# Memory norm, keys and values of two attention layers moved ahead of the first feed-forward

## The chip, the cores and the metric

One core of a Trainium2 chip runs the whole kernel. Its engines work side by side, each through its own queue of instructions in order: TensorE (matmuls), VectorE, ScalarE, GpSimd and SyncE (SP, which only issues DMAs). They wait for each other and for transfers by semaphores. The metric is the time of one execution on the device in microseconds; lower is better.

## The reference

The input is 512 tokens of width 1024. A first block adds a mixer of four branches and a feed-forward of width 4096, both behind norms with shift and scale from a conditioning vector. A second block of two layers follows. Each of its layers reads, beside the tokens, a fixed memory of 256 tokens:

```python
for layer in range(DEPTH_2):
    xn = rmsnorm(h, norm_mix[layer])
    mn = rmsnorm(mem, norm_mem[layer])
    ...                     # q, k, v, qm from xn; mix = attention of 12 heads
    mem_out = memory_attention(split_heads(qm, N_MEM_HEADS), mn, w_mem_kv[layer])
    heads = jnp.concatenate([mix, mem_out], axis=1)
    h = h + merge_heads(heads) @ w_out[layer]
    h = h + conv_ffn(rmsnorm(h, norm_ffn[layer]), w_up[layer], conv_w[layer],
                     conv_b[layer], w_down[layer])

def memory_attention(qm, mem_n, w_mem_kv):
    km, vm = jnp.split(mem_n @ w_mem_kv, 2, axis=-1)
    ...                     # softmax(qm km / sqrt(64)) vm, 4 heads of 64
```

`mem` does not depend on `x`. Layer 0 uses attention with forget gates, layer 1 a dilated attention with rotated queries and keys.

## The kernel before

Activations lie transposed: channels on the 128 partitions, tokens along the row, in 8 blocks (`KT`). Weights come as a stream of 334 pieces of 128x1024, one per output tile of 128 channels. Each matmul operand is split in a high and a low part, so a product of one block is three matmuls (high with high, high with low, low with high) and a tile is 24 matmuls of 512 columns. For the memory the columns are 256.

**Weights.** GpSimd loads them into four slots. `load_high(q)` waits until an older piece has been used (`w_used`) and issues a 512 KB DMA. `load_low(q)` waits for that to land, writes its negative into `w_lo`, and issues a second 512 KB DMA that adds the full weights to it. In the queue, `load_high(q + 2)` stands between `load_low(q)` and `load_low(q + 1)`. TensorE's `open_piece` waits for the low part. The order of pieces is fixed by `layout`.

**TensorE's order** is written out by hand: `project(tiles, owner, ...)` makes tiles one after the other in four PSUM banks in turn; `owner` names the semaphore that says when a bank has been read. `modulation(g)` is eight one-column matmuls that sum a weight column over partitions. `total_squares` is one matmul with ones, which sums squares for a norm.

**Between mixer and feed-forward.** VectorE's `mixer_update(k)` adds output tile k to x and then calls `modulate`, which scales two pieces of the modulation weights (`in_ada`, 512 KB each, 16 of them here, brought by SP into four slots, each when the piece four before it has been used). When all are through, TensorE makes `modulation(4)` and the sum of squares, ScalarE the root (`rms_x`), VectorE the reciprocal (`norm_start`) and the eight blocks of the norm, which ScalarE (high part) and VectorE (low part) finish, and the first feed-forward tile follows.

**The memory.** SP loads it (1 MB, `memT`) once before the attention of layer 0 and again after it, into the room of the softmax rows. In the last group of the first feed-forward, and in the last group of layer 0's, ScalarE squares it, VectorE adds the squares, and one `total_squares` sums them. In the head of each attention layer VectorE makes the norm (`memory_norm`: three operations per block, 24 in all), and TensorE makes two key tiles and two value tiles (`HEAD_PIECES`: memq0, memq1, q0, k0, v0, memk0, memk1, memv0, memv1). Values must have tokens on the partitions, so `turn` transposes each value tile with TensorE into bank 7 from a copy by ScalarE (`value_copy`), and VectorE takes it (`value_taken`). In layer 0 VectorE then turns the forget logits into running sums (`forget_parts`). Only when the last memory value has been taken does `attention` begin: 32 units (8 of the memory heads first), each with scores, row maximum, exponent, division, transpose and output, with the remaining 15 projections fed in between. Units of 12 heads read the forget rows that SP copies to `g_lo`.

## Time and profile before

| | |
|---|---|
| time, median of 3 runs | 2319.56 us (2309.91 to 2321.72) |
| span of the profiled execution | 2315.7 us |
| TensorE busy | 2147.8 us, 93% |
| VectorE, ScalarE, GpSimd busy | 56%, 20%, 37% |
| mean granted TensorE clock | 0.957 of full |
| DMA | 393.60 MB, mean 170 GB/s |

The profile has several views. The page gives the busy time of each engine and the chain of work that ended last. The chain of waits goes back from the last instruction to what released each. The timeline lists instructions with the idle time before each and what ended it. The windows give busy times, the granted clock and DMA traffic of a stretch. Times are microseconds from the start of the span.

### The profile page before, as it was taken

The numbers are of one execution on the slowest core, as the hardware profiler recorded it, in microseconds if no ns is written. First come the engines' busy times: TensorE is split into PE (matmuls) and PEld (weight loads), VectorE is DVE, ScalarE is ACT, GpSimd is POOL, SyncE is SP. The second block draws the span as 40 slices with busy tenths as digits, with TensorE's granted clock in tenths as the row PEclk, the third lists the DMA queues.
The fourth block names the chain that finished last, engine by engine and source line by source line (L and its number), as shares of the span: only waits on it lengthen the run. The fifth ranks groups of instructions, "written<-read, shape, count | busy, mean of one in ns | idle before, by whom it ended". The sixth has DMA issues, their size and how long they took to land.

```text
span 2315.7 us, 27377 instructions
## 1 busy us (share of the span) xinstructions
PE 2147.8 (93%) x10790; PEld 1703.9 (74%) x10790; DVE 1296.3 (56%) x1824; ACT 456.1 (20%) x839; POOL 846.9 (37%) x1009
## 2 busy tenths in 40 slices
PE   6889798998799999989989999999899989999996
PEld 5668586676588888866767878787766668878784
DVE  6775655436763243674444745637636747727274
ACT  2112301210100000313342211113133432102011
POOL 1323233232244444432214444444432224444442
PEclk7999899997799999999999999999999989999998
DMA  8867577576799999985528989898965449899885
GB/s 280 221 141 167 114 151 145 121 181 161 229 236 196 196 192 193 192 174 115 108 57 194 194 184 195 179 200 187 197 136 101 92 102 186 178 198 191 184 193 141
DMA packets 121783, 393.60 MB, mean 170 GB/s; under 512 B 25220, under 2 KB 27396, under 8 KB 121272
## 3 DMA queue, kind: packets, MB, share of 16 engines
q0 software_dynamic: 96624, 350.46, 71.3%
q1 hardware_dynamic: 25032, 41.39, 5.6%
q8 instruction: 86, 1.41, 0.3%
q14 instruction: 41, 0.34, 0.1%
HBM read 387.92 MB, written 3.92 MB: 169 GB/s over the span
## 4 chain that ended last, share of the span: by engine, by line
PE 74%; DVE 14%; DMA 7%; issue 2%; ACT 1%; POOL 1%; SPq 0%; DVEq 0%; ACTq 0%; POOLq 0%
PE ps L1582 62%; DMA w_lo<-in_w 4%; PE ps L1710 2%; DMA arena<-in_ada 2%; PE ps L1611 2%; PE ps L1739 2%; PE ps L1725 1%; DVE work L668 1%; PE ps L1896 1%; DVE g_lo L462 1%; POOL w_lo L429 1%; DVE arena L556 1%; DVE arena L669 1%; DMA w_hi<-in_w 1%; DVE small L855 1%
## 5 line engine op out<-in xcount | busy, mean ns | idle before, releaser
L1582 PE MATMUL ps<-h_hi,w_hi 128*128 128x512 f32 x1760 | 711.1, 404 | 27.1 <-DVE h_lo L512 13.3
L1582 PE MATMUL ps<-h_hi,w_lo 128*128 128x512 f32 x1760 | 690.1, 392 | 0.0
L1582 PE MATMUL ps<-h_lo,w_hi 128*128 128x512 f32 x1760 | 690.0, 392 | 0.0
L424 POOL DMA_DIRECT2D w_hi<-in_w x334 | 187.4, 561 | 1289.9 <-PE ps L1582 1203.3
L1582 PEld LDWEIGHTS ps<-h_hi,w_hi 128*128 128x128 f32 x1760 | 332.6, 189 | 126.2 <-issue 29.9
L1582 PEld LDWEIGHTS ps<-h_hi,w_lo 128*128 128x128 f32 x1760 | 332.8, 189 | 71.3
L1582 PEld LDWEIGHTS ps<-h_lo,w_hi 128*128 128x128 f32 x1760 | 333.4, 189 | 64.8 <-issue 2.2
L429 POOL TENSOR_SCALAR w_lo<-w_hi 128x1024 fp32r<-128x1024 f32 x334 | 359.5, 1076 | 45.3 <-DMA w_hi<-in_w 39.8
L1582 PE MATMUL ps<-g_hi,w_hi 128*128 128x512 f32 (+1 forms) x792 | 313.8, 396 | 28.6 <-DMA w_lo<-in_w 19.5
L432 POOL DMA_DIRECT2D w_lo<-in_w x334 | 301.0, 901 | 106.0 <-POOL w_lo L429 106.0
L1582 PE MATMUL ps<-g_lo,w_hi 128*128 128x512 f32 (+1 forms) x792 | 307.1, 388 | 0.0
L1582 PE MATMUL ps<-g_hi,w_lo 128*128 128x512 f32 (+1 forms) x792 | 306.8, 387 | 0.0
L1582 PEld LDWEIGHTS ps<-g_hi,w_hi 128*128 128x128 f32 x792 | 153.0, 193 | 66.8 <-DMA w_lo<-in_w 24.9
L1582 PEld LDWEIGHTS ps<-g_hi,w_lo 128*128 128x128 f32 x792 | 153.1, 193 | 29.8
L1582 PEld LDWEIGHTS ps<-g_lo,w_hi 128*128 128x128 f32 x792 | 153.3, 194 | 28.2 <-issue 0.5
L1540 ACT ACTIVATE arena<-arena,vec 128x512 f32<-128x512 f32 x88 | 71.8, 816 | 404.6 <-DVE arena L901 401.4
L915 DVE TENSOR_TENSOR x<-ps,x 128x512 f32<-128x512 f32 x48 | 33.2, 692 | 170.2 <-PE ps L1582 159.1
L906 DVE SCALAR_TENSOR_TENSOR arena<-arena,vec 128x511 f32<-128x511 f32 x88 | 115.4, 1311 | 3.3 <-ACT arena L1540 0.3
L901 DVE TENSOR_TENSOR arena<-ps,work 128x512 f32<-128x512 f32 x88 | 60.9, 692 | 89.9 <-PE ps L1582 88.5
L1170 DVE TENSOR_TENSOR arena<-arena 128x512 f32<-128x512 f32 x32 | 51.4, 1606 | 72.2 <-ACT arena L1461 72.2
L1178 DVE SCALAR_TENSOR_TENSOR x<-ps,mod,x 128x512 f32<-128x512 f32 x32 | 24.0, 751 | 102.2 <-PE ps L1582 102.1
L461 DVE CAST g_hi<-arena 128x512 fp32r<-128x512 f32 (+1 forms) x100 | 76.3, 763 | 3.4
(373 smaller groups left out, 2080.1 us busy)
## 6 DMA issues: line engine op xcount, KB each, us to landing
w_hi<-in_w POOLq DMA_DIRECT2D x334, 512.0 KB, 4.0
w_lo<-in_w POOLq DMA_DIRECT2D x334, 512.0 KB, 5.8
arena<-in_ada SPq DMA_DIRECT2D x40, 512.0 KB, 9.4
x<-in_ada SPq DMA_DIRECT2D x8, 512.0 KB, 7.9
x<-in_xT SPq DMA_DIRECT2D x1, 2048.0 KB, 10.0
x<-in_xT SPq DMA_DIRECT2D x4, 512.0 KB, 4.4
arena<-in_memT SPq DMA_DIRECT2D x2, 1024.0 KB, 7.1
out_y<-arena SPq DMA_DIRECT2D x4, 512.0 KB, 2.6
```

Of the source, the lines that this page charges most:

```text
L424: pool.dma_start(w_hi[:, q % SLOTS, :], A["w"][q]).then_inc(S(f"high_in{q % SLOTS}"), 16)
L429: pool.tensor_scalar(w_lo[:, q % SLOTS, :], w_hi[:, q % SLOTS, :].bitcast(F32), -1.0, 0.0, ALU.mult, ALU.add).then_inc(S("negated"), 1)
L432: pool.dma_start(w_lo[:, q % SLOTS, :], A["w"][q], accum_op=ALU.add).then_inc(S(f"low_in{q % SLOTS}"), 16)
L461: do(dve.tensor_copy(hi, src))
L901: do(dve.tensor_tensor(cv_m["z"][:, side, :], tile()[:], rstd, ALU.mult), "conv_scaled")
L906: do(dve.scalar_tensor_tensor(dst[:, 1:], z[:, :T - 1], w(1), dst[:, 1:], ALU.mult, ALU.add))
L1170: do(dve.tensor_tensor(s, r, r, ALU.mult), "relu_used")
L1540: do(act.activation(c[:, j % 2, :], cv_m["z"][:, side, :], ACT.Identity, scale=V("cw2", at), bias=V("cb2", 44 * layer + 22 * side + j0 + j ...
L1582: mm = pe.matmul(bank, w[:, slot, cols], a(k), start=(k == 0 and i == 0), stop=(k == blocks - 1 and i == 2))
L1611: mm = pe.matmul(banks[i], w[:, slots[i], cols], a(k), start=(k == 0 and j == 0), stop=(k == blocks - 1 and j == 2))
L1710: mm = pe.matmul(ps[2 + g][:, 0:width], at_m["q"][half(g), pair, P * qb:P * qb + P], keys, start=True, stop=not fox)
L1739: mm = pe.matmul(ps[6][64 * g:64 * g + 64, P * qb:P * qb + P], values, at_m["pt"][:, u % 2, g, P * b:P * b + P], start=(b == 0), stop=(b = ...
```

## The change

The memory norm, keys and values of both layers are made once, between the output projection of the mixer and the first feed-forward. Their eight weight pieces move to that place in the stream; the number of pieces stays 334.

- SP loads the memory once, behind four modulation pieces and before x is loaded again.
- ScalarE makes eight squares (128x256), TensorE adds them up by eight matmuls with ones, before the output projection. ScalarE then writes 16 high parts (memory times gain), VectorE 16 low parts, three per `mixer_update`. The norm's root is not applied to them: keys are multiplied by it on VectorE, in the first feed-forward group; for values it is brought from a row to a column (`diag`, `mem_row`) and given as the scale of ScalarE's copy.
- Values are made with the memory as the stationary operand and the weights as the moving one (`memory_values`), so they come out with tokens on the partitions, and are not transposed.
- The heads of the attention lose the memory norm and four tiles. The transpose of v0 moves into the first unit.

```diff
-HEAD_PIECES = ["memq0", "memq1", "q0", "k0", "v0", "memk0", "memk1", "memv0", "memv1"]
+HEAD_PIECES = ["memq0", "memq1", "q0", "k0", "v0"]
...
             for q in range(24, 24 + ADA):
                 ada_piece(q, ada_m["ada"])
+            sp.dma_start(mem_in, A["memT"]).then_inc(S("mem_in"), 16)
...
-            sp.wait_ge(S("ada_used"), 48 - ADA_PE)
-            sp.dma_start(mem_in, A["memT"]).then_inc(S("mem_in"), 16)
             sp.wait_ge(S("forget_parts"), 1)
-            sp.wait_ge(S("taken"), TURNED[0].index("memv1") + 1)
+            sp.wait_ge(S("x_done"), 8 + 8 * FF_GROUPS)
...
             sp.wait_ge(S("heads"), NP + NMP)
-            sp.dma_start(mem_in, A["memT"]).then_inc(S("mem_in"), 16)
             sp.dma_start(masks, A["mask_dil"]).then_inc(S("mask_in"), 16)
... VectorE
             def memory_root():
+
                 need("rms_ready")
                 do(dve.reciprocal(mem_rstd, mem_rstd))
+                for i in range(2):
+                    do(dve.tensor_tensor(mem_m["diag"], mem_rstd[:, P * i:P * i + P], K("ident"), ALU.mult))
+                    do(dve.tensor_reduce(mem_row[:, i:i + 1], mem_m["diag"], AX.X, ALU.add), "mem_row")
+
+            def memory_low(i):
+
+                layer, k = i // KT, i % KT
+                need("mem_high")
+                do(dve.scalar_tensor_tensor(mn(g_lo, layer, k), mem_in[:, k, :], V("g_mem2", 8 * layer + k), mn(g_hi, layer, k).bitcast(F32),
+                                            ALU.mult, ALU.subtract), "mem_ready")
...
-                for k in range(KT):
-                    memory_norm(k)
...
-                value_scaled("v0")
-                for i in range(NMP):
-                    do(dve.tensor_copy(km[:, i, :], tile()[:, 0:MT]), "dve_freed")
-                    if i == 0:
-                        value_taken("v0")
...
-                skip(2)
-                for i in range(NMP):
-                    value_taken(f"memv{i}")
+                value_scaled("v0")
...
             def mixer_update(k):
                 do(dve.scalar_tensor_tensor(x[:, k, :], tile()[:], mod[:, 16 + k:17 + k], x[:, k, :], ALU.mult, ALU.add), "x_done")
+                for i in range(3 * k, min(3 * k + 3, 2 * KT)):
+                    memory_low(i)
+                if k == 2:
+                    memory_root()
                 modulate(3 + k // 4, 2 * (k % 4), 2 * (k % 4) + 2)
...
-                    if last:
-                        add_square(j, mem_sq, mem_total)
+                    if first and j < 2 * NMP:
+                        keys = mem_keys[j // NMP][:, j % NMP, :]
+                        dve.wait_ge(S("mem_copied"), 2 * N_KV)
+                        do(dve.tensor_tensor(keys, keys, mem_rstd, ALU.mult), "mem_scaled")
... ScalarE
+            act.wait_ge(S("mem_in"), 16)
+            for k in range(KT):
+                if k >= MEM_SQ:
+                    act.wait_ge(S("mem_square_used"), k - MEM_SQ + 1)
+                do(act.activation(mem_sq(k), mem_in[:, k, :], ACT.Square), "mem_square")
+            act.wait_ge(S("tile"), n.value["tile"])
+            for layer in range(2):
+                for k in range(KT):
+                    do(act.activation(mn(g_hi, layer, k), mem_in[:, k, :], ACT.Identity, scale=V("g_mem2", 8 * layer + k)), "mem_high")
+            act.wait_ge(S("mem_square_used"), KT)
+            do(act.activation(mem_rstd, PB[:, 0:MT], ACT.Sqrt, bias=small[:, 38, 0:1], scale=1.0 / D), "rms_ready")
             skip(8)
             rms_x(0)
-            high_shifted(lambda k: mod[:, 24 + k:25 + k])
+            for i in range(NMP):
+                keys_copy(0, i)
+            values_copy(0)
...
+            for k in range(KT):
+                high2(k)
+                if k in (1, 3):
+                    keys_copy(1, k // 2)
+            values_copy(1)
... TensorE
+            for k in range(KT):
+                pe.wait_ge(S("mem_square"), k + 1)
+                pe.matmul(PB[:, 0:MT], K("ones"), mem_sq(k), start=(k == 0), stop=(k == KT - 1)).then_inc(S("mem_square_used"), 1)
             project(7, "x_done", ready=lambda k: need("merged"))
             modulation(3)
             project(1, "x_done")
+            pe.wait_ge(S("mem_ready"), 2 * KT)
+            project(1, "mem_copied", operand=memory[0], width=MT)
             modulation(4)
+            total_squares(work[:, 2, :])
+            project(NMP - 1, "mem_copied", operand=memory[0], width=MT)
+            memory_values(0)
+            project(NMP, "mem_copied", operand=memory[1], width=MT)
+            memory_values(1)
...
-            total_squares(work[:, 2, :])
...
-                project(1, "dve_freed", operand=mem, width=MT, ready=lambda k: need("mem_ready"))
-                turn("v0", layer)
-                project(NMP - 1, "dve_freed", operand=mem, width=MT)
-                for i in range(NMP):
-                    project(1, "v_copied", operand=mem, width=MT)
-                    if i:
-                        turn(f"memv{i - 1}", layer)
-                turn(f"memv{NMP - 1}", layer)
-                attention(layer)
+                attention(layer, ready)
```

In three places the order of instructions shows what moves. The first is TensorE at the end of the output projection, before (L1647 is the modulation sum, L1663 the sum of squares, the rows behind them the first feed-forward tile):

```order
L1582 MATMUL ps<-h_lo,w_hi 128x512
L1582 MATMUL ps<-h_hi,w_lo 128x512
L1647 MATMUL ps<-con,arena 128x1 x8
L1663 MATMUL ps<-work,con 128x512
L1582 MATMUL ps<-h_hi,w_hi 128x512
```

The same place now. The rows from the first piece are the end of memk0 of layer 0, in the second the first values of the memory (L1681) follow memk1:

```order
L1585 MATMUL ps<-g_lo,w_hi 128x256
L1585 MATMUL ps<-g_hi,w_lo 128x256
L1650 MATMUL ps<-con,arena 128x1 x8
L1666 MATMUL ps<-work,con 128x512
L1585 MATMUL ps<-g_hi,w_hi 128x256
```

```order
L1585 MATMUL ps<-g_hi,w_hi 128x256
L1585 MATMUL ps<-g_lo,w_hi 128x256
L1585 MATMUL ps<-g_hi,w_lo 128x256
L1681 MATMUL ps<-w_hi,g_hi 128x256
L1681 MATMUL ps<-w_lo,g_hi 128x256
L1681 MATMUL ps<-w_hi,g_lo 128x256
```

One memory tile stands before the modulation, seven behind it and before the feed-forward tile. The second place is VectorE in the same stretch, before (L1153 adds a tile to x, L556 scales modulation weights):

```order
L1153 SCALAR_TENSOR_TENSOR x<-ps,mod,x 128x512
L556 SCALAR_TENSOR_TENSOR arena<-arena,small 128x1024 x2
L469 TENSOR_TENSOR work<-work 128x512
L1153 SCALAR_TENSOR_TENSOR x<-ps,mod,x 128x512
L556 SCALAR_TENSOR_TENSOR arena<-arena,small 128x1024 x2
```

and now, at the third tile (L506 is `memory_low`, L497 to L500 `memory_root`, L566 scales modulation weights):

```order
L1137 SCALAR_TENSOR_TENSOR x<-ps,mod,x 128x512
L506 SCALAR_TENSOR_TENSOR g_lo<-arena,vec,g_hi 128x256 x3
L497 RECIPROCAL arena<-arena 128x256
L499 TENSOR_TENSOR arena<-arena,con 128x128
L500 TENSOR_REDUCE small<-arena 128x1
L499 TENSOR_TENSOR arena<-arena,con 128x128
L500 TENSOR_REDUCE small<-arena 128x1
L566 SCALAR_TENSOR_TENSOR arena<-arena,small 128x1024 x2
```

The memory's low parts stand between the update of x and the modulation weights. The third place is TensorE in the head of layer 0. Before, the end of memv1 and its transposes (L1676) stand ahead of the first scores (L1710):

```order
L1582 MATMUL ps<-g_lo,w_hi 128x256
L1582 MATMUL ps<-g_hi,w_lo 128x256
L1676 MATMUL ps<-con,arena 128x128 x4
L1710 MATMUL ps<-arena 128x256 x4
L1582 MATMUL ps<-h_hi,w_hi 128x512
```

Now the end of v0 stands there, and the transposes of v0 (L1701) come in the first unit:

```order
L1585 MATMUL ps<-h_lo,w_hi 128x512
L1585 MATMUL ps<-h_hi,w_lo 128x512
L1737 MATMUL ps<-arena 128x256 x4
L1585 MATMUL ps<-h_hi,w_hi 128x512
...
L1701 MATMUL ps<-con,arena 128x128 x4
L1752 MATMUL ps<-con,arena 128x128 x4
```

The scores follow v0 directly.

## Rows read from the trace of the kernel before

**Rows 1.** The page, parts 1 and 4: engines, and the chain that ended last.

```profile
PE 2147.8 (93%) x10790; PEld 1703.9 (74%) x10790; DVE 1296.3 (56%) x1824; ACT 456.1 (20%) x839; POOL 846.9 (37%) x1009
...
PE 74%; DVE 14%; DMA 7%; issue 2%; ACT 1%; POOL 1%; SPq 0%; DVEq 0%; ACTq 0%; POOLq 0%
```

**Rows 2.** Chain of waits, mixer to feed-forward: start, duration, what released the next.

```profile
598.78 10.76 DMA arena<-in_ada
...
609.63 1.28 DVE arena L556
...
611.11 3.57 PE ps L1647 x16
614.68 1.93 PE ps L1663 x2
...
617.48 3.37 DVE work L505
...
627.53 57.14 PE ps L1582 x234
```

**Rows 3.** Windows: busy time of each engine (instructions), clock, DMA share, GB/s.

```profile
610.00:615.00 5.00, 3.89 (x17) 3.89 (x18) 2.54 (x6) 0.00 (x0) 0.00 (x0) 0.50 1.01 339
...
1035.00:1040.00 5.00, 2.85 (x23) 2.40 (x21) 4.17 (x7) 0.38 (x1) 2.33 (x3) 1.00 1.01 214
1040.00:1045.00 5.00, 1.30 (x6) 0.61 (x6) 0.89 (x3) 2.41 (x5) 0.00 (x0) 0.51 0.66 113
...
1620.00:1625.00 5.00, 4.52 (x21) 3.41 (x20) 3.69 (x5) 2.24 (x4) 2.95 (x4) 1.00 0.90 208
```

**Rows 4.** Timeline of layer 0's head: start, duration, engine, line, [idle before].

```profile
1008.26 1.42 DVE L761 SCALAR_TENSOR_TENSOR arena<-ps,work 128x512 f32<-128x512 f32 x2
...
1017.44 0.39 PE L1582 MATMUL ps<-h_hi,w_lo 128*128 128x512 f32 x1
...
1031.03 1.77 DVE L823 TENSOR_SCALAR work<-work 12x512 f32<-12x512 f32 x1
...
1037.94 0.68 DVE L832 TENSOR_TENSOR work<-work 12x512 fp32r<-12x512 f32 x1
...
1041.64 0.69 DVE L855 TENSOR_REDUCE small<-ps 128x2 f32<-128x512 f32 x1 [1.48 <-PE ps L1710]
```

**Rows 5.** Timeline of layer 1's head: rotation of k0, first row maximum.

```profile
1668.17 1.02 PE L1673 MATMUL ps<-arena,con 128*128 128x512 f32 x2
...
1691.48 0.69 DVE L855 TENSOR_REDUCE small<-ps 128x2 f32<-128x512 f32 x1 [1.19 <-PE ps L1710]
```

**Rows 6.** Chain of waits at the mixer's end: low weights land, three tiles.

```profile
496.61 8.95 DMA w_lo<-in_w
...
505.59 16.62 PE ps L1582 x72
```

**Rows 7.** Chain of waits, both heads: transposes of v0, memory tiles.

```profile
1024.61 1.11 PE ps L1676 x4
...
1676.91 0.23 PE ps L1582
...
1685.32 3.13 PE ps L1582 x24
```

**Rows 8.** Timeline: the column sum of the memory's squares.

```profile
1607.07 0.59 PE L1663 MATMUL ps<-arena,con 128*128 128x256 f32 x2
```

**Rows 9.** Timeline: ScalarE's first square of x, VectorE's first memory operation.

```profile
566.54 0.63 ACT L1231 ACTIVATE work<-x 128x512 f32<-128x512 f32 x1 [42.12 <-issue]
...
1009.71 0.48 DVE L801 SCALAR_TENSOR_TENSOR arena<-arena,vec 128x256 f32<-128x256 f32 x1
```

**Rows 10.** Timeline of GpSimd: loads of high weights, first and last of five.

```profile
1619.85 0.55 POOL L424 DMA_DIRECT2D w_hi<-in_w  x1 [1.09 <-PE ps L1582]
...
1639.87 0.56 POOL L424 DMA_DIRECT2D w_hi<-in_w  x1 [1.84 <-PE ps L1582]
```

**Rows 11.** Windows: beside the four modulation pieces at the mixer's end.

```profile
495.00:498.00 3.00, 3.00 (x15) 2.49 (x14) 2.93 (x3) 0.00 (x0) 1.90 (x2) 1.00 0.97 354
```

More of the change, by code:

```diff
@@ L136, in turned_pieces @@
 def turned_pieces(layer):
-    return [name for name in HEAD_PIECES + BESIDE_PIECES if name[0] == "v" or name[:4] == "memv" or (layer and name[0] in "qk")]
+    return [name for name in HEAD_PIECES + BESIDE_PIECES if name[0] == "v" or (layer and name[0] in "qk")]
 TURNED = [turned_pieces(layer) for layer in range(2)]
@@ L169, in bank_of @@
         return tile % BANKS
-    pieces = n_block1 + sum(n + N_KV + 8 + 2 * FF2 + 8 * len(FF2_GROUPS) for n in (N_FOX, N_DIL))
+    pieces = n_block1 + sum(n + 8 + 2 * FF2 + 8 * len(FF2_GROUPS) for n in (N_FOX, N_DIL))
     with ExitStack() as ctx:
@@ L1663, in total_squares, with memory_values @@
                 pe.matmul(bank[:, 0:width], K("ones"), acc, start=True, stop=True).then_inc(S("squares_total"), 1)
+            def memory_values(layer):
+                at = [bank_of(t[0] + i) for i in range(2)]
+                for b in at:
+                    pe.wait_ge(S(freed[b][0]), freed[b][1])
+                for k in range(KT):
+                    if k % 4 == 0:
+                        slot = open_piece()
+                    hi, lo = mn(g_hi, layer, k), mn(g_lo, layer, k)
+                    cols = slice(MT * (k % 4), MT * (k % 4) + MT)
+                    for i in range(2):
+                        tokens = slice(P * i, P * i + P)
+                        for j, (a, w) in enumerate(((hi, w_hi), (hi, w_lo), (lo, w_hi))):
+                            mm = pe.matmul(ps[at[i]][:, 0:NMP * P], a[:, tokens], w[:, slot, cols], start=(k == 0 and j == 0),
+                                           stop=(k == KT - 1 and j == 2))
+                            if k % 4 == 0 and i == 0 and j == 0:
+                                mm.then_inc(S("w_used"), 1)
+                        if k == KT - 1:
+                            mm.then_inc(S("tile"), 1)
+                            freed[at[i]] = ("mem_copied", n.next("mem_copied"))
+                t[0] += 2
             def turn(name, layer):
                 i, base = TURNED[layer].index(name), TURNED_BASE[layer]
[L1668 removed]
+                kind = lambda other: "rope_copied" if other[0] in "qk" else "v_scaled"
                 pe.wait_ge(S(kind(name)), sum(kind(other) == kind(name) for other in sum(TURNED[:layer], []) + TURNED[layer][:i + 1]))
@@ L1708, in scores @@
                     for g in range(2):
-                        keys = at_m["k"][half(g), pair, 0:width] if pair < NP else at_m["km"][half(g), pair - NP, :]
+                        keys = at_m["k"][half(g), pair, 0:width] if pair < NP else mem_keys[layer][half(g), pair - NP, :]
                         mm = pe.matmul(ps[2 + g][:, 0:width], at_m["q"][half(g), pair, P * qb:P * qb + P], keys,
@@ L2029, in _ @@
                     two_products(pairs, *g, "x_done", hidden)
-                    if layer == 0 and group == len(FF2_GROUPS) - 1:
-                        total_squares(mem_total, MT)
                     project(6, "x_done", operand=g, blocks=pairs)
@@ L2104, in layout @@
     stream.append(pieces_of(first["w_o"]))
+    for layer in range(2):
+        kv = i["w_mem_kv_2"][layer]
+        stream += [pieces_of(kv[:, :NMP * P]), kv[:, NMP * P:].reshape(2, 4, P, NMP * P).transpose(0, 2, 1, 3).reshape(2, P, D)]
     for g in range(FF_GROUPS):
```

111 lines of the change are left out of this document (45 added, 66 removed).

## The prediction

> **What bounds the kernel now.** I read the page first: TensorE is busy 93% of the span, and one matmul line is most of the chain that ended last [rows 1]. So only what opens or closes an idle stretch of TensorE moves the end. The chain of waits and the timeline show three such stretches that the change touches. The first lies between the mixer's output projection and the feed-forward. The last modulation weight is used up at 609.63 + 1.28 = 610.9 us, sixteen small matmuls and the sum of squares follow until 616.6, then a square root and a reciprocal, and the first feed-forward tile is fed block by block until the unbroken run that starts at 627.53 [rows 2]. The clock falls to its lower level there, 0.50 in the windows [rows 3]. The other two are the heads of the attention layers. VectorE makes the memory norm there, and TensorE has 256-column products and transposes between the last value projection and the first scores: 1017.8 to 1041.6 in layer 0 [rows 4], 1669.2 to 1691.5 in layer 1 [rows 5]. The change takes the memory work out of the second and third and puts it in the first.
>
> **Gain 1, the head of layer 0.** The first row maximum of the scores starts at 1041.64 [rows 4]. Afterwards v0 still ends about 1017.8, its last matmul going out at 1017.44, and the first scores can follow it. VectorE then decides. The memory queries are scaled at 1009.7 and q0 right behind them. k0's tile ends one tile pitch, 16.62 / 3 = 5.54 us [rows 6], before v0, so it is scaled at about 1013. Behind it the forget chain stands unchanged, from 1031.03 to 1037.94 + 0.68, so 7.6 us [rows 4], and then v0's scaling, 0.7. That is 1013.0 + 7.6 + 0.7 = 1021.3: the forget chain takes the memory norm's place. Gain 1041.6 − 1021.3 = **20.3 us**. Bounds 18 (k0 half a tile later) and 21.5 (the chain's first step took 1.77 us, its neighbours under 0.7 for the same shape).
>
> **Gain 2, the head of layer 1.** The first row maximum starts at 1691.48. The rotation of k0 on TensorE ends at 1668.17 + 1.02 = 1669.2 [rows 5]. VectorE then has its three operations and v0's scaling, four of 0.7 us, so 1672.1. Gain **19.4 us**, bounds 18 and 20.
>
> **What the attention gets in return.** The transpose of v0 now stands in the first unit. Four such transposes took 1.11 us at the lower clock [rows 7], about half at the higher. TensorE is packed in the later units, so I charge 0.6 per layer, **1.2 us**. The value transposes of the memory are inside the gains. Of the column sums of the memory's squares two go, shown at 0.59 us each [rows 8]: **−1.0 us** in all. Eight of that width come in before the output projection, at most 4.7 us. I take them as free: TensorE is fed block by block by VectorE there, and ScalarE is idle for 42.12 us before its first square [rows 9], which holds 8 squares and 16 scaled copies of some 0.5 us each, 12 us. Were that cover gone, they would cost the 4.7.
>
> **Cost 1, VectorE during the output projection.** It gets 16 operations of 128x256 at 0.48 us [rows 9], a reciprocal of half the width of one that took 3.37 us [rows 2], and four short ones: some 11 us. Part of that falls in waits for modulation weights. But each of their transfers starts only when a slot has been used, and lands 10.76 us later [rows 2], so a late use is a late landing. Walking the sixteen pieces through with that latency, the modulation ends 4.5 us later, at about 615.5. Bounds 2 and 7.
>
> **Cost 2, eight more tiles in the first stretch.** Before, the 234 matmuls end at 627.53 + 57.14 = 684.7 [rows 2]. Nine whole tiles at 5.5 back from there, the first feed-forward tile ends at 635.2. Afterwards TensorE has one keys tile in the idle time, a wait to 615.5, then modulation and squares, 3.57 + 1.93 at the lower clock [rows 2] and half of it at the higher, so about 620. Then come seven memory pieces and the feed-forward tile. 24 matmuls of 256 columns take 3.13 us [rows 7], so the matmuls alone would be through by 642, the feed-forward tile by 647. What decides is the weights, since a memory piece brings as many bytes as any other and has half the matmul time. In layer 1's head a load is released at 1676.91, when the piece two ahead starts, and its own matmuls start at 1685.32 [rows 7]: 8.4 us for two pieces, 4.2 each. In the tail of the last feed-forward group, where many loads follow each other, five loads of high weights are issued between 1619.85 and 1639.87 [rows 10], 5.0 us apart, with the DMA engines 90% busy [rows 3]. I take 4.6 per piece, the middle, since the first of the seven are half loaded and the later ones queue. The feed-forward tile then starts at 620 + 7 x 4.6 = 652, less about 1.5 for the pieces already there, and ends at 656. Cost 656 − 635 = **21 us**, cost 1 within it. Bounds: 12 (matmul time alone, 647) and 26 (5.0 per piece, VectorE at its worst bound). ScalarE puts its copies of keys and values among the norm's high parts. Behind the second keys copy it has four of these to make, some 7 us with VectorE's steps between them, and TensorE has two value pieces for as long, so the norm stays covered.
>
> **Cost 3, the memory load beside the mixer's end.** The 1 MB transfer now queues on SP behind four modulation pieces. Low weights took 8.95 us to land there and TensorE waited for them [rows 6], at 354 GB/s [rows 11]. At that rate 1 MB is 3.0 us. The stretch behind it has some slack, so **1.5 us**, bounds 0 and 3.5. The second memory load, at the end of layer 0, goes. TensorE hardly waits for weights there: 0.3 us gained.
>
> **The sum.** 20.3 + 19.4 + 1.0 + 0.3 − 1.2 − 21 − 1.5 = 17.3 us gained. Against the profiled span of 2315.7 that gives 2298.4. The median of the timed runs lies 3.9 us above that span: 2319.6 − 17.3 = **2302.3 us**.
>
> **Rivals.**
> (a) The supply is no limit: pieces come 4.0 us apart or less and the clock is back at once. The first stretch costs 14, the gain is 24, the time 2295 us. For it: the 8.4 us for two pieces. Against it: only four memory pieces stood in a row there.
> (b) The stretch is dearer: 5.0 or more per piece, VectorE 7 us late, and the memory load costs 3.5. Then 26 + 3.5 leave a gain of 10, 2309 us. For it: modulation pieces of the last group load beside the weights until about 620.
> (c) Bursts at the lower clock. TensorE works 3.1 of 4.6 us while it waits for weights. If the clock stayed at its lower level, a piece would take 5.2 us, which hides the supply, and the stretch would cost 0.5 x 7, some 3 us more: 2306. Against it: the clock was 1.00 in a window with 2.85 of 5 us busy and fell only in the next, with 1.30 [rows 3].
> The Trainium skill, "TensorE: Matmul & The Clock Gate", section "HAM oscillation — how this bites in real kernels", has a kernel whose bursts behind DMA waits each start at the lower clock. [...]
> (d) Slower. The four weight slots work as one: in GpSimd's queue the low part of a piece waits behind the high load of the next, which waits for a piece to start, so every piece pays the whole 8.4 us of the layer 1 row. The tile then starts at 620 + 7 x 8.4 = 679 and ends at 684, a cost of 49, 2330 us. It decides from 6.9 us per piece, where the stretch costs the 38 us that are gained elsewhere. Against it: in the row itself two pieces were under way, and the tail shows 5.0.
> (e) The attention doesn't start earlier, held by a bank, by q0 or by the forget rows. The memory units use no forget rows, and banks 2 and 3 are free when q0 and k0 are scaled, by 1013. Ten us later in both layers than I say, and 2322 is the time.
>
> **How the numbers follow.** The forecast, a gain of 13 to 21 us: 0.53. (a) 0.15, (b) 0.16, (c) 0.07, (d) 0.04, (e) 0.05. A measurement of this kernel can tell about 0.5%, 11.6 us, from no change. Faster by more: the forecast, (a), (c) and a little of (b), 0.77. Within it: most of (b) and (e), 0.18. Slower: the worst of (d) and (e), 0.05. The range from 2293 to 2311 takes in the forecast, (c), nearly all of (a) and most of (b). Its ends are the bounds of the supply and of the memory load.
>
> **What would show it.** Right: the first feed-forward tile ends near 656; memory pieces start 4.2 to 5.0 us apart, waiting for low weights; the modulation ends near 615; the first row maxima come some 20 us earlier, counted from the last v0 matmul. Wrong: an unbroken run from 642 (a), pieces over 7 us apart (d), ScalarE's high parts ending last before the feed-forward, or scores that wait for something other than VectorE's scaling of v0.

## The result: 0.5% faster, near what was forecast

The changed kernel takes 2302.67 us (median of 7 runs, 2298.59 to 2311.46), beside 2318.42 us for the kernel before (7 runs, 2309.91 to 2321.72). The ratio is 0.9945, with a 95% interval of 0.993 to 0.996. The forecast was 2302.3 us. A second measurement of the same kernel gave 0.9947 (0.9928 to 0.9967). Taken as a ratio, the gain is 12.8 us (9 to 16), less than the 17.3 us of the sum.

In the profiled executions the spans are 2300.9 us after and 2315.7 us before. The page's parts 1 and 4, the rows that answer [rows 1]:

```profile
PE 2139.9 (93%) x10794; PEld 1703.4 (74%) x10794; DVE 1272.2 (55%) x1775; ACT 462.3 (20%) x850; POOL 850.3 (37%) x1009
...
PE 77%; DVE 12%; DMA 7%; issue 1%; ACT 1%; POOL 1%; SPq 0%; DVEq 0%; ACTq 0%; POOLq 0%
```

TensorE is busy for 7.9 us less and the span is 14.8 us shorter, so about half of the gain is idle time that went. VectorE's share of the chain fell from 14% to 12%.

**The heads gave what they were to give.** Timeline of VectorE and TensorE in layer 0's head, of the changed kernel (start, duration, engine, line, operation, [idle before]). These rows answer [rows 4]:

```profile
1037.59 0.39 PE L1585 MATMUL ps<-h_hi,w_lo 128*128 128x512 f32 x1
...
1033.37 1.81 DVE L813 TENSOR_SCALAR work<-work 12x512 f32<-12x512 f32 x1
...
1039.43 0.68 DVE L822 TENSOR_TENSOR work<-work 12x512 fp32r<-12x512 f32 x1
1040.14 0.69 DVE L788 TENSOR_TENSOR arena<-ps,work 128x512 f32<-128x512 f32 x1
1040.87 0.69 DVE L843 TENSOR_REDUCE small<-ps 128x2 f32<-128x512 f32 x1
```

The first row maximum (L843) starts 1040.87 − 1037.98 = 2.9 us behind the end of v0's last matmul. Before it was 1041.64 − 1017.83 = 23.8. That is 20.9 us gained. In all eleven profiles of the changed kernel and its variants this distance is 2.7 to 2.9 us. As forecast, the forget chain (L813 to L822) and v0's scaling (L788) now decide. In layer 1, the rows that answer [rows 5]:

```profile
1671.51 1.02 PE L1698 MATMUL ps<-arena,con 128*128 128x512 f32 x2
...
1674.84 0.69 DVE L788 TENSOR_TENSOR arena<-ps,work 128x512 f32<-128x512 f32 x1
1675.57 0.69 DVE L843 TENSOR_REDUCE small<-ps 128x2 f32<-128x512 f32 x1
```

From the end of k0's rotation to the row maximum it is 3.0 us (in all eleven profiles), where it was 22.3: 19.3 us gained.

**The first stretch took over half of it.** Chain of waits of the changed kernel from the modulation to the first feed-forward tile (start, duration, what released the next), which answers [rows 2]:

```profile
599.62 12.11 DMA arena<-in_ada
...
611.83 1.28 DVE arena L566
...
613.30 1.95 PE ps L1650 x16
615.25 1.33 PE ps L1666 x2
...
619.04 6.66 DMA w_lo<-in_w
...
626.46 5.89 DMA w_hi<-in_w
...
633.94 7.38 DMA w_lo<-in_w
...
644.68 5.34 DMA w_lo<-in_w
650.02 0.04 issue
650.06 10.04 PE ps L1585 x43
```

Before, this chain ran through the norm on VectorE. Now it is mostly a chain of weight loads. TensorE's timeline shows the same from its side. Seven tiles follow the first piece behind the modulation: six of the memory and the first of the feed-forward. Five of them start with a wait for low weights.

```profile
625.74 0.42 PE L1681 MATMUL ps<-w_hi,g_hi 128*128 128x256 f32 x1 [2.24 <-DMA w_lo<-in_w]
635.67 0.39 PE L1585 MATMUL ps<-g_hi,w_hi 128*128 128x256 f32 x1 [2.35 <-DMA w_lo<-in_w]
641.46 0.36 PE L1681 MATMUL ps<-w_hi,g_hi 128*128 128x256 f32 x1 [1.16 <-DMA w_lo<-in_w]
645.05 0.38 PE L1681 MATMUL ps<-w_hi,g_hi 128*128 128x256 f32 x1 [0.48 <-DMA w_lo<-in_w]
650.06 0.50 PE L1585 MATMUL ps<-h_hi,w_hi 128*128 128x512 f32 x1 [1.89 <-DMA w_lo<-in_w]
```

The seven memory pieces behind the modulation start at 615.65, and the feed-forward tile at 650.06: (650.06 − 615.65) / 7 = 4.9 us for each. Windows of the same stretch (busy time of each engine, granted clock, DMA share, GB/s):

```profile
620.00:630.00 10.00, 7.76 (x53) 7.55 (x52) 2.32 (x3) 0.38 (x1) 4.98 (x6) 0.83 0.97 224
630.00:640.00 10.00, 7.65 (x51) 7.43 (x50) 7.33 (x8) 4.23 (x7) 5.21 (x6) 0.83 0.95 230
640.00:650.00 10.00, 6.54 (x51) 5.95 (x49) 6.18 (x7) 4.22 (x7) 5.34 (x6) 1.00 0.91 189
```

The DMA engines are over nine tenths busy and TensorE is not. From the last matmul of the output projection to the first feed-forward tile's start it is 650.06 − 606.10 = 44.0 us. Before it was 635.2 − 5.5 − 607.06 = 22.6, with the tile's end as the prediction worked it out: 21.4 us dearer.

**The books of the two traces.** In the profiled execution of the changed kernel the recurrence in front ended 4.1 us earlier (−4.1), though no edit touches what runs before it. Then: the mixer's end +3.1, the first stretch +21.4, layer 0's head −20.9, layer 0 from the first scores to layer 1's rotation +4.1, layer 1's head −19.3, the rest +1.1. That makes −14.6; the spans differ by 14.8. The −4.1 and the +4.1 are taken up below, at the changed kernel's second measurement.

### The profile page after: what moved, and what is told of

Read it like the earlier page. It is cut to its first block, busy times and chain, and to the rows that moved or that the text cites. A ratio compares the mean times of both kernels' runs of the same rounds, so it can differ in the third digit from the quotient of the medians.

```text
span 2300.9 us, 27327 instructions
## 1 busy us (share of the span) xinstructions
PE 2139.9 (93%) x10794; PEld 1703.4 (74%) x10794; DVE 1272.2 (55%) x1775; ACT 462.3 (20%) x850; POOL 850.3 (37%) x1009
## 3 DMA queue, kind: packets, MB, share of 16 engines
q0 software_dynamic: 96624, 350.46, 70.6%
## 4 chain that ended last, share of the span: by engine, by line
PE 77%; DVE 12%; DMA 7%; issue 1%; ACT 1%; POOL 1%; SPq 0%; DVEq 0%; ACTq 0%; POOLq 0%
PE ps L1585 64%; DMA w_lo<-in_w 4%; PE ps L1737 2%; PE ps L1614 2%; PE ps L1766 2%; PE ps L1752 1%; DMA arena<-in_ada 1%; DVE work L678 1%; PE ps L1924 1%; DMA w_hi<-in_w 1%; POOL w_lo L428 1%; DVE arena L566 1%; DMA x<-in_xT 1%; DVE arena L679 1%; DVE work L468 1%
## 5 line engine op out<-in xcount | busy, mean ns | idle before, releaser
L1585 PE MATMUL ps<-g_hi,w_hi 128*128 128x512 f32 (+1 forms) x760 | 305.8, 402 | 27.8 <-DMA w_lo<-in_w 20.7
L1585 PE MATMUL ps<-g_lo,w_hi 128*128 128x512 f32 (+1 forms) x760 | 299.5, 394 | 0.0
L1585 PE MATMUL ps<-g_hi,w_lo 128*128 128x512 f32 (+1 forms) x760 | 299.2, 394 | 0.0
L1585 PEld LDWEIGHTS ps<-g_hi,w_hi 128*128 128x128 f32 x760 | 147.6, 194 | 64.9 <-DMA w_lo<-in_w 24.9
L1585 PEld LDWEIGHTS ps<-g_hi,w_lo 128*128 128x128 f32 x760 | 147.5, 194 | 30.4
L1585 PEld LDWEIGHTS ps<-g_lo,w_hi 128*128 128x128 f32 x760 | 148.1, 195 | 29.1 <-issue 0.8
L1476 ACT ACTIVATE arena<-ps 128x512 f32<-128x512 f32 x32 | 19.2, 600 | 289.6 <-PE ps L1585 289.6
```

Source lines behind the costliest of these rows:

```text
L1585: mm = pe.matmul(bank, w[:, slot, cols], a(k), start=(k == 0 and i == 0), stop=(k == blocks - 1 and i == 2))
```

## Experiments

All ratios are to the kernel before, run beside it on the same chip, with 95% intervals. The gain against the changed kernel is (0.9946 − ratio) x 2316 us, 0.9946 being the mean of its two measurements.

| kernel | median us | ratio | less than changed kernel, us |
|---|---|---|---|
| changed kernel, again | 2301.61 | 0.9947 (0.9928 to 0.9967) | 0 |
| no_pieces | 2283.02 | 0.9869 (0.985 to 0.9888) | 17.8 |
| no_loads | 2292.66 | 0.9908 (0.9887 to 0.9929) | 8.8 |
| few_matmuls | 2303.78 | 0.9955 (0.9942 to 0.9969) | −2.1 |
| half_low | 2297.38 | 0.9918 (0.9893 to 0.9943) | 6.5 |
| mem_late | 2298.72 | 0.9929 (0.9912 to 0.9946) | 3.9 |
| keys_first | 2295.46 | 0.9916 (0.9902 to 0.9931) | 6.9 |
| lows_early | 2302.73 | 0.9945 (0.9927 to 0.9963) | 0.2 |
| two_edits | 2295.55 | 0.9904 (0.988 to 0.9929) | 9.7 |
| all_three | 2296.75 | 0.992 (0.9905 to 0.9935) | 6.0 |

### Loads or matmuls? no_pieces, no_loads, few_matmuls

The theory (W): the weight supply sets the pace of the stretch. The rivals: TensorE's matmuls, some at the lower clock, set it (M), or the norm on VectorE and ScalarE does (N). no_loads takes the eight memory pieces' weights out of the stream and runs all matmuls on weights that lie in a slot already (the part for the values is shown):

```diff
-                    if k % 4 == 0:
-                        slot = open_piece()
+                    slot = (piece[0] - 1) % SLOTS
```

few_matmuls keeps all loads and runs one of eight blocks of 128 rows of each keys piece, and two of the eight of each pair of values pieces:

```diff
-                for k in range(KT):
+                for k in (0, 4):
```

no_pieces does both.

> The changed kernel without the eight memory pieces of the weight stream, and with 3 or 6 matmuls per memory tile instead of 24; everything else (squares, high and low parts, copies, banks) stays. It leaves out the memory's keys and values, so its time shows what the pieces cost and nothing of the result. Theory W (the stretch is paced by weights): the first feed-forward tile is then held by the norm alone, whose last block follows the modulation (613.3) by some 24 us, so the tile ends near 640 instead of 655.5, and the time falls by 13 to 18 us against the changed kernel, to 2285 to 2290. Rival N (ScalarE's copies among the high parts hold the norm, which was complete only at 647.9): the tile ends at 650 or later, and the time falls by less than 6 us.

> The changed kernel with all memory matmuls, which read the slot of the last output projection piece instead of weights of their own; eight pieces fewer are loaded. Its keys and values are wrong, the work on TensorE is the same. Theory W: memory tiles follow each other every 3.1 us from 615.7 (lower clock at the start apart), are done by 640, and the feed-forward tile ends at 645 to 648: 8 to 11 us less than the changed kernel, 2292 to 2295. Rival M (matmul time and the lower clock are the cost, weights are not): within 3 us of the changed kernel, 2300 to 2303. Rival N: likewise, since the copies stay.

> The changed kernel with all eight memory pieces loaded and opened, but 3 to 6 matmuls per tile instead of 24. It leaves out most of the memory's products. Theory W: the pace stays about 4.9 us per piece, since the slots and transfers set it, and the first feed-forward matmul starts at 648 to 651 as in the changed kernel: 0 to 2 us less, 2301 to 2303. Rival M: the seven tiles shrink by 2.7 us each and the time falls by 12 to 18 us, to 2285 to 2291.

> The changed kernel unchanged, as the reference of this call. All theories: 2302.7, within 3 us, ratio to the kernel before about 0.994. Its profile shows which stretches vary from one execution to the next: the 4.1 us by which the part before the memory load was shorter in the first profile, and the tail of the last feed-forward group of layer 0, which was 3.5 us longer there, should both move if they are chance.

The second profile of the changed kernel answers in part. The stretch from layer 0's first row maximum to the end of layer 1's rotation took 627.2 us, where the first profile has 631.7 and the kernel before 627.6. Over all twelve profiles it lies between 624.2 and 633.7, so the +4.1 of the books is chance. The long matmul run behind the recurrence began at 487.8, again early. But over the eleven profiles of the changed kernel and its variants its start lies between 486.9 and 495.7, on both sides of the 491.6 of the kernel before. So the −4.1 is within the spread between executions as well.

Without most of the matmuls nothing was gained; without the loads 8.8 us were. TensorE's timeline of few_matmuls:

```profile
626.97 0.58 PE L1687 MATMUL ps<-w_hi,g_hi 128*128 128x256 f32 x1 [6.18 <-DMA w_lo<-in_w]
632.26 0.58 PE L1585 MATMUL ps<-g_hi,w_hi 128*128 128x256 f32 x1 [3.64 <-DMA w_lo<-in_w]
636.64 0.58 PE L1585 MATMUL ps<-g_hi,w_hi 128*128 128x256 f32 x1 [3.38 <-DMA w_lo<-in_w]
641.01 0.55 PE L1687 MATMUL ps<-w_hi,g_hi 128*128 128x256 f32 x1 [3.36 <-DMA w_lo<-in_w]
646.80 0.58 PE L1687 MATMUL ps<-w_hi,g_hi 128*128 128x256 f32 x1 [4.17 <-DMA w_lo<-in_w]
650.88 0.79 PE L1585 MATMUL ps<-h_hi,w_hi 128*128 128x512 f32 x1 [2.43 <-DMA w_lo<-in_w]
```

(650.88 − 626.97) / 5 = 4.8 us per piece with TensorE nearly idle. That is the price of the loads by themselves. Now one window of few_matmuls and one of no_loads:

```profile
620.00:650.00 30.00, 7.73 (x28) 6.00 (x27) 16.69 (x18) 8.90 (x16) 17.31 (x20) 0.50 0.96 215
```

```profile
620.00:640.00 20.00, 20.00 (x166) 19.91 (x166) 14.40 (x17) 8.05 (x15) 0.00 (x0) 1.00 0.01 2
```

In the first the DMA engines are 96% busy. In the second TensorE is busy without a gap at the full clock, its tiles follow 2.9 us apart, and the feed-forward tile starts at 639.42, after 34.6 us from the output projection's end. In no_pieces the feed-forward is back in the hands of the norm, as before the change. Its matmuls wait for VectorE's low parts, and the unbroken run of the feed-forward begins at 634.30, 27.6 us behind the projection's end, where it was 20.5 in the kernel before. The changed kernel starts its first feed-forward tile after 44.0 us. So the norm isn't its limit, and N falls. It isn't far behind, though. In the changed kernel its last low parts are done at 647.9, 2.1 us before that tile starts, and in few_matmuls, with fewer matmuls ahead of its copies, at 644.5:

```profile
645.44 2.49 DVE L522 SCALAR_TENSOR_TENSOR h_lo<-work,mod,h_hi 128x512 fp32r<-128x512 f32 x2
```

### Bytes or round trip? half_low

```diff
-                pool.dma_start(w_lo[:, q % SLOTS, :], A["w"][q], accum_op=ALU.add).then_inc(S(f"low_in{q % SLOTS}"), 16)
+                part = D // 2 if n_mixer + 8 <= q < n_mixer + 8 + 2 * N_KV else D
+                pool.dma_start(w_lo[:, q % SLOTS, 0:part], A["w"][q][:, 0:part], accum_op=ALU.add).then_inc(S(f"low_in{q % SLOTS}"), 16)
```

> The changed kernel, but for the eight pieces of memory weights the load of the low part covers only half of its columns, so half of the low parts are wrong; all matmuls and all high loads stay. Theory B (the loads of the low parts, which add to what is in the tile, take most of the 4.9 us per piece: with the high parts at the 382 GB/s of the plain queue 1.4 us, the adding loads 3.3 to 3.5 us): a piece every 3.2 to 3.4 us, now bound by the 24 matmuls of 3.1 us, the first feed-forward tile starts 10 to 12 us earlier, and the time falls by 8 to 12 us. Rival S (the pace is a round trip of issue, landing, negation and second issue over four slots, and not bytes): the pace stays above 4.3 us and the time falls by less than 4 us.

The gain of 6.5 us lies between the two expectations, and its interval, from about 1 to 12 us, takes in both. From the projection's end to the first feed-forward tile it is 42.2 us, where four profiles with all the bytes have 46.4 in the mean (below). The pace of the pieces tells more, and it is at the edge of S's. Four of its tile starts, all with a wait for low weights, from its timeline:

```profile
636.80 0.39 PE L1586 MATMUL ps<-g_hi,w_hi 128*128 128x256 f32 x1 [1.10 <-DMA w_lo<-in_w]
641.19 0.38 PE L1586 MATMUL ps<-g_hi,w_hi 128*128 128x256 f32 x1 [1.26 <-DMA w_lo<-in_w]
645.62 0.35 PE L1682 MATMUL ps<-w_hi,g_hi 128*128 128x256 f32 x1 [1.30 <-DMA w_lo<-in_w]
649.85 0.39 PE L1682 MATMUL ps<-w_hi,g_hi 128*128 128x256 f32 x1 [1.12 <-DMA w_lo<-in_w]
```

They are 4.35 us apart. The DMA view's queue rows (packets, MB, share of the 16 engines' time) give the price of a MB. First GpSimd's queue in the changed kernel, then in half_low, both from 630 to 652 us:

```profile
q0 software_dynamic: 1257, 4.57, 92.5%
```

```profile
q0 software_dynamic: 1449, 3.98, 81.7%
```

That is 0.925 x 22 / 4.57 = 4.45 us per MB, and 0.817 x 22 / 3.98 = 4.52. A MB costs the same though in half_low two thirds of it are high parts and not one half. So the adding load isn't the dear one, and theory B's split fails. A whole piece of 1.05 MB holds the DMA engines for 4.7 of its 4.9 us. A piece of three quarters would hold them for 3.5, yet comes every 4.35, with the engines at 0.85 in its windows. So a second limit stands right behind the bytes. What it is, no run shows. By the program's order high load, negation, low load and the slot's release follow each other, so a chain of waits between TensorE, GpSimd and the DMA is a candidate.

### The memory load beside the mixer's end: mem_late

```diff
+            sp.wait_ge(S("rw_o"), 1)
             sp.dma_start(mem_in, A["memT"]).then_inc(S("mem_in"), 16)
```

> One edit: SyncE waits until the mixer's output projection has begun (rw_o) before it issues the load of the memory, which then falls at about 526 us, where the DMA engines stand idle; nothing else moves. Theory L (the memory's bytes are what made the wait for the low weights near 503 us grow from 1.43 to 2.86 us and what let TensorE's clock drop behind it): the wait is back at 1.2 to 1.7 us, the 72 matmuls behind it take 16.6 us again, and the time falls by 1.4 to 3 us against the changed kernel. Rival A (the wait is due to the modulation vectors' loads just ahead, or differs from kernel to kernel by the place of things in memory): the wait stays at 2.4 to 2.9 us and the time moves by less than 1 us. Rival B (the load now comes too late for the sum of squares or for the memory keys): a new wait of VectorE or ScalarE for the memory, and a time up by 1 us or more.

The changed kernel waited here, from TensorE's timeline; the row answers [rows 6]:

```profile
502.93 0.69 PE L1585 MATMUL ps<-h_hi,w_hi 128*128 128x512 f32 x1 [2.86 <-DMA w_lo<-in_w]
```

In mem_late there is no wait at all between 489.73 and 519.00: 126 matmuls in 29.3 us, where the changed kernel took 33.6 and the kernel before 30.6. The same holds in the other two kernels with the late load, all_three and two_edits, where these matmuls take 29.1 and 29.2 us. In the eight profiles with the load in its place they take 32.0 to 33.6, in the mean 33.1. So the memory's bytes made the wait; the modulation pieces, which are still there, leave at most the 1.43 us of the kernel before's profile. The windows show it, the changed kernel's first, then mem_late's:

```profile
500.00:505.00 5.00, 2.14 (x6) 1.69 (x6) 3.20 (x3) 1.88 (x2) 2.41 (x4) 0.81 1.05 238
505.00:510.00 5.00, 5.00 (x20) 3.99 (x20) 0.00 (x0) 0.00 (x0) 1.66 (x2) 0.85 0.93 214
```

```profile
500.00:505.00 5.00, 5.00 (x23) 3.88 (x22) 4.86 (x5) 1.88 (x2) 3.40 (x4) 1.00 0.93 205
505.00:510.00 5.00, 5.00 (x23) 4.11 (x23) 1.22 (x1) 0.60 (x1) 2.97 (x4) 1.00 1.00 215
```

The clock falls with the wait, too. Of the 3.9 us between the two groups, part has gone by the end of the output projection. From the start of the long matmul run (487.51 in the changed kernel) to the end of the projection (606.10) it is 115.4 us before. The eight profiles with the load in its place show 115.5 to 118.6, 117.3 in the mean. The three with it late show 113.9 to 115.8, 114.8 in the mean. The load costs 1.9 us against the single profile of the kernel before, and placing it late is worth 2.4 (from unrounded means). The timed gain of 3.9 us agrees within its interval.

### Where the stretch starts: keys_first, lows_early

keys_first puts all of layer 0's keys tiles ahead of modulation(4), into TensorE's wait for VectorE:

```diff
-            project(1, "mem_copied", operand=memory[0], width=MT)
+            project(NMP, "mem_copied", operand=memory[0], width=MT)
             modulation(4)
             total_squares(work[:, 2, :])
-            project(NMP - 1, "mem_copied", operand=memory[0], width=MT)
```

(NMP is 2 and a tile is one piece, so a layer has two tiles of keys and one of them moves. The expectation below counts four and three, and so does that of two_edits; it should say two and one. Its time was worked out from the wait that is filled and not from that count.)

lows_early makes eight of the sixteen low parts of the memory before VectorE waits for the projection's first tile, and moves the memory's root behind the norm's:

```diff
+            for i in range(KT):
+                memory_low(i)
+            lows = [8, 10, 12, 13, 14, 15, 16, 16, 16]
...
-                for i in range(3 * k, min(3 * k + 3, 2 * KT)):
+                for i in range(lows[k], lows[k + 1]):
                     memory_low(i)
-                if k == 2:
-                    memory_root()
```

> One edit: on TensorE all four tiles of layer 0's memory keys stand ahead of the modulation(4) columns, in the place where TensorE waited 2.85 us for VectorE, instead of one tile ahead and three behind. Theory W (a new piece of weights every 4.9 us paces the stretch, whatever TensorE does): the chain of pieces starts some 4 us earlier, so the first feed-forward tile begins at 646 to 647 us instead of 650.06, and the time falls by 3 to 4.5 us. Rival V (VectorE's norm work decides when the feed-forward can begin, and the modulation now starts 1 us later): the first feed-forward matmuls wait for the rounding of h and the time moves by less than 1.5 us, or rises.

> One edit, on VectorE alone: eight of the sixteen low parts of the memory are made before VectorE waits for the mixer's last output, the others one or two at a time between the updates, and the memory's root stands behind the root of the feed-forward norm. Theory V (VectorE's memory work delays the modulation(4) columns by 3.1 us and with them everything behind): modulation starts 3 us earlier and so does the first feed-forward tile; the time falls by about 3 us. Rival W2 (the memory keys behind the modulation wait for their own weights and not for VectorE, so an earlier modulation buys only what the slots of weights allow): the first piece behind it moves by 3 us, but later ones keep the pace of the loads and the time falls by 0 to 1.5 us.

keys_first gained 6.9 us, more than W's 3 to 4.5, though the intervals allow 4. Its one moved tile starts at 612.24, again with a wait for weights, so that even the earlier start ran into the supply:

```profile
612.24 0.38 PE L1585 MATMUL ps<-g_hi,w_hi 128*128 128x256 f32 x1 [3.27 <-DMA w_lo<-in_w]
```

The stretch from the projection's end is 43.4 us in it. In the four profiles of kernels with all loads and the changed kernel's order (changed kernel twice, few_matmuls, mem_late) it is 44.0, 48.1, 46.0 and 47.3, in the mean 46.4. So the edit saves 3.0 there, as W said. The other two kernels with this edit, all_three and two_edits, have 42.8 and 44.1, so the mean of the three, 43.4, says the same. What else is in the 6.9 I can't show.

lows_early gained nothing. Its modulation did start sooner: 6.6 us behind the projection's end, where seven profiles with the changed order show 7.2 to 9.2, 8.1 in the mean, and the kernel before 4.1. That is 1.5 us sooner, half of the 3 that the expectation counted on. But the stretch stayed at 47.0. TensorE's next tiles took the wait over:

```profile
611.50 3.49 PE L1652 MATMUL ps<-con,arena 128*128 128x1 f32 x16 [2.36 <-DVE small L567]
...
632.35 0.58 PE L1587 MATMUL ps<-g_hi,w_hi 128*128 128x256 f32 x1 [4.20 <-DMA w_lo<-in_w]
...
642.87 0.55 PE L1683 MATMUL ps<-w_hi,g_hi 128*128 128x256 f32 x1 [3.12 <-DMA w_lo<-in_w]
```

Theory V's 3 us did not come, and W2 agrees with what did: an earlier modulation bought nothing while the pieces came at the pace of their loads. With 1.5 us moved and an interval of some 4 us to either side, V isn't excluded by the time alone; the waits above speak against it.

### Together: all_three, two_edits

> The three edits together. If they act in different places, the gains add up: 8 to 10 us less than the changed kernel, about 2293 us. If keys first and lows early are two ways to start the same chain of pieces earlier, the second brings nothing more, and the time is 5 to 7 us under the changed kernel. Less than 4 us would say that the stretch is set by something that none of the three moves.

> The changed kernel with the late memory load and with all four tiles of layer 0's memory keys ahead of modulation(4), and without the earlier low parts, which brought nothing alone (2302.73 us). If the other two act in different places (the wait near 503 us, and the start of the chain of weight pieces at 612 us), the gains of 3.9 and 7 us, taken as ratios to the kernel before, come nearly together: 2290 to 2294 us. If they share one bound, the DMA engines, which are fully busy from 575 to 615 us in all versions, the time is no better than keys first alone: 2295 to 2297 us.

two_edits, late load and keys first, has the lowest ratio of the kernels that compute the whole result, 0.9904: 9.7 us under the changed kernel where the single gains of 3.9 and 6.9 add to 10.8. By the ratio it is nearly additive; but its median, 2295.55, is that of keys_first alone, and the intervals overlap, so the runs don't settle it. all_three, at 6.0 us, is no better than keys_first alone; with the low parts early as well nothing is added. Both are faster than the kernel before. The interval of two_edits ends where that of the changed kernel's second measurement begins (0.9929, 0.9928), and all_three's overlaps it.

## Why the prediction came out right, step by step

**Gain 1 and gain 2 were right.** 20.3 forecast and 20.9 measured; 19.4 and 19.3. The distances are the same in every profile, so this is no luck. The step that carried them, to ask which of VectorE's operations is late once the memory work is gone, named the right one both times. Rival (e) is out.

**Cost 2's mechanism was right, its size a little low.** This is the term of the sum that was mis-sized most. The weights decide, 4.9 us per piece where I took 4.6. The middle between 4.2 and 5.0 was the wrong choice. The 4.2 came from two pieces with idle time ahead of them [rows 7], and the 5.0 from a stretch where the DMA engines were as busy [rows 3, 10]: the row with the same load was the one to take. The first feed-forward tile ends at about 650.06 + 5.6 = 655.7, forecast 656, but the execution ran 4.1 us early, so in the clock of before this is 660. Of the 4 us, 3.1 are the mixer's end. Over four profiles the stretch is 46.4 − 22.6 = 23.8 us dearer, not 21; rival (a) is out, rival (b) took the right direction. The norm stayed covered, as said, but by 2.1 us only.

**Cost 1 was the right size and the wrong cause to worry about.** The modulation waits 8.1 − 4.1 = 4.0 us longer in the mean of seven profiles, 3.1 in the profiled run; 4.5 was forecast. But by lows_early this wait isn't what the time hangs on. It also isn't VectorE alone. Its last steps wait for modulation weights to land:

```profile
605.46 1.28 DVE L566 SCALAR_TENSOR_TENSOR arena<-arena,small 128x1024 f32<-128x1024 f32 x1 [1.76 <-DMA arena<-in_ada]
...
611.83 1.28 DVE L566 SCALAR_TENSOR_TENSOR arena<-arena,small 128x1024 f32<-128x1024 f32 x1 [1.86 <-DMA arena<-in_ada]
```

**Cost 3**, 1.5 forecast. The one profile says 3.1 and the mean of eight 1.9. A single trace would have told me that this term was wrong by a factor of two, when most of that was its spread of 3 us between executions.

**The clock, rival (c), half happened, and no cost of it can be seen.** The windows above show 0.83, 0.83 and 1.00. The tile that starts at 625.74, after an idle 2.24 us, runs at the lower level from its first matmul, 0.42 us for one where the higher gives 0.28. The tile at 635.67, after 2.35, begins at the higher level and falls to the lower one 0.5 us later. Those at 641.46 and 645.05, after 1.16 and 0.48 us of idle, stay at the higher. The idle time just before doesn't decide it alone: a tile of keys_first, at 624.87 after 2.50 us, stays at the higher level too. The two slow tiles take 4.6 us each, which still fits into a pitch of 4.9. In mem_late one takes 5.5 (from 632.39, slow to its end), the next follows without a wait, and the one behind waits 2.04 us for its weights all the same. Of the four profiles with the changed order, the one with these two has the shortest stretch, 44.0; that of after_again, with one such tile, has 48.1. I priced (c) at 3 us more, for pieces of 5.2 us against 4.6 (that is 0.6 for each and 4 us in all, not the 0.5 that I took). No run kept all pieces at the lower clock with all their matmuls; few_matmuls, at 0.50 all through, has too few matmuls to price it. The Trainium skill, "TensorE: Matmul & The Clock Gate", section "HAM oscillation — how this bites in real kernels", has a kernel in which waits for DMA of some 3 to 5 us make each burst start at the lower clock. The waits here are shorter, and one of the four bursts above starts at it.

**The small terms.** v0's transposes, now in the first units, were charged at 0.6 us each and took nearly twice that. TensorE had idled 5.54 us shortly before, and the granted clock was 0.50 from 1044 to 1049:

```profile
1044.15 1.22 PE L1737 MATMUL ps<-arena 64*128 64x256 f32 x4 [5.54 <-ACT arena L1513]
...
1048.03 1.05 PE L1701 MATMUL ps<-con,arena 128*128 128x128 f32 x4
```

With layer 1's 1.05 this is 2.1 us, not 1.2. The eight new column sums run from 548.63 to 552.24, ahead of two tiles that then wait 1.67 us each for VectorE's low parts. They were as good as free: from the end of the 126 matmuls to the end of the projection it is 83.0 to 86.7 us in the eleven profiles with them, 84.6 in the mean, and 84.8 in the kernel before. The second memory load of the kernel before was issued at 1220.22, at the end of layer 0's attention. Behind it TensorE waits for weights once, and in the changed kernel not at all up to 1241:

```profile
1231.62 0.50 PE L1582 MATMUL ps<-g_hi,w_hi 128*128 128x512 f32 x1 [0.19 <-DMA w_lo<-in_w]
```

So 0.3 us for the missing load was the right size.

**The sum again, with measured terms:** 20.9 + 19.3 + 0.2 − 23.8 − 1.9 − 2.1 + 1.0 = 13.6 us, the last term, for the two column sums that went, being the forecast's own. The ratio says 12.8. The forecast's 17.3 was too high by about 4, of which 2.8 are the piece pitch and what hangs on it. That the time itself fell so close, 2302.67 to 2302.3, is luck: the kernel before came out 1.1 us faster beside it than its first median, and the rest is the spread of the medians, where the difference of the two (15.8 us) is itself 3 us over what the ratio gives.

The slower rival (d), a full round trip of 8.4 us per piece, did not happen: the pitch is 4.9. The 4.35 of half_low, which bytes don't explain, lies near half of 8.4, as two overlapping round trips would give; that is a guess, and no run shows it.

## What to carry to other kernels

Work moved out of an idle gap must be priced by the resource that is scarce in its new place. Here the matmuls were cheap and the weights that came with them set the time, at nearly the pace, 4.9 to 5.0 us, that the tail of layer 0 had shown with the DMA engines as full. Take a pace from a row with the same load and not from the middle of two. And before shortening a wait, ask what the next piece waits for: the edit that shortened the visible wait on VectorE brought nothing, the one that started the loads' consumers earlier brought several us.

## What the runs showed of the hardware that I had not expected

**A full DMA share doesn't mean one rate.** In the windows from 590 to 600 us of the changed kernel, and from 620 to 630, the share is 1.06 and 0.97, the rates 325 and 224 GB/s:

```profile
590.00:600.00 10.00, 9.14 (x47) 7.45 (x45) 9.58 (x12) 1.27 (x2) 4.32 (x5) 1.00 1.06 325
```

The difference is whose loads they are. The DMA view of the kernel before from 560 to 575 us has both queues side by side, GpSimd's (q0, weights) and SyncE's (q1, modulation weights and x):

```profile
q0 software_dynamic: 380, 1.42, 40.9%
q1 hardware_dynamic: 504, 1.81, 34.5%
```

Per MB that is 0.409 x 15 / 1.42 = 4.3 us for GpSimd's and 0.345 x 15 / 1.81 = 2.9 for SyncE's, with packets of the same size, 3.7 and 3.6 KB. GpSimd's packets take half as long again. The changed kernel has 4.5 and 3.1 in the same window, and the page of the kernel before gives 0.713 x 2315.7 / 350.46 = 4.7 and 0.056 x 2315.7 / 41.39 = 3.1 over the whole span. GpSimd's loads also differ in kind: all of them go from float32 into tiles declared float32r, and every second one adds. By the Trainium skill, "DMA: Bandwidth & Descriptors", section "SWDGE vs HWDGE vs iDMA", loads that add or that cast can be issued from GpSimd alone; whether the cast is what makes them slow no run here shows.

**Loads that add cost no more than GpSimd's loads that don't**: 4.45 and 4.52 us per MB, where half and where about one third of the bytes are added.

**One execution differs from the next by more than the terms in question.** The stretch from the matmul run to the projection's end took 115.5 to 118.6 us over eight profiles with the memory load in its place, and layer 0 up to layer 1's rotation 624.2 to 633.7 over twelve. A term of 1 to 3 us can't be read from one trace, unless it is a distance like those in the heads, which came out within 0.2 us each time.
